# A hybrid encoder layer on one core: how the row maxima of the attention get from columns into the score product

## The reference, cut to what matters

```
def one_block(qi):                                   # 128 queries
    s = jnp.einsum('bkgqd,bskd->bkgqs', qi, kh)      # scores against all keys
    p = jax.nn.softmax(s, axis=-1)
    return jnp.einsum('bkgqs,bskd->bqkgd', p, vh)
```

## Time and profile before

| | |
|---|---|
| median of three runs | 3463.08 us |
| profiled execution, its own time | 3468.2 us |
| span of its trace | 3466.0 us |
| TensorE matmul busy | 2960.6 us, 85% |
| VectorE busy | 2319.8 us, 67% |
| ScalarE busy | 1557.6 us, 45% |
| GpSimd busy | 582.9 us, 17% |
| mean granted TensorE clock | 0.921 |

### The profile page before, as it was taken

The page is one execution under the profiler, slowest core; times in us unless marked ns, Lnnn a source line. Parts: engine busy times, 40 slices in busy tenths (PEclk is TensorE's granted clock), DMA queues, the critical chain, the costliest instruction groups (busy, mean ns, idle before and its releaser), DMA issues. The chain is left out here.

```text
span 3466.0 us, 42658 instructions
## 1 busy us (share of the span) xinstructions
PE 2960.6 (85%) x13075; PEld 2028.4 (59%) x13075; DVE 2319.8 (67%) x2874; ACT 1557.6 (45%) x1980; POOL 582.9 (17%) x395
## 2 busy tenths in 40 slices
PE   6999999669999999996996499959999999999940
PEld 3666666434444444443664277847777777777730
DVE  2556555427777777774776544458888788888856
ACT  2323322102333333335553223217777777777744
POOL 0000000000000000002893000012323232332335
PEclk8999999768999999998997699969999999999975
DMA  6112111353111101100003433346677776678347
GB/s 245 49 46 63 49 45 47 95 160 86 29 28 36 33 21 36 33 16 7 1 0 128 135 121 124 124 163 253 219 270 264 294 278 237 224 260 314 144 161 313
DMA packets 237754, 446.17 MB, mean 129 GB/s; under 512 B 21377, under 2 KB 95197, under 8 KB 236925
## 3 DMA queue, kind: packets, MB, share of 16 engines
q1 hardware_dynamic: 222277, 397.67, 34.3%
q0 software_dynamic: 15408, 47.73, 3.6%
q10 hardware_dynamic: 8, 0.01, 0.0%
HBM read 367.45 MB, written 86.29 MB: 131 GB/s over the span
## 5 line engine op out<-in xcount | busy, mean ns | idle before, releaser
L2175 DVE TENSOR_TENSOR weights_rest<-w,weights_rounded 128x2048 fp32r<-128x2048 f32 x315 | 716.8, 2289 | 134.8 <-ACT weights_rounded L2108 132.5
L2108 ACT ACTIVATE weights_rounded<-w 128x2048 fp32r x315 | 602.1, 1921 | 171.9 <-PE ps_up L2030 108.4
L832 ACT ACTIVATE probs<-ps_scores 128x1024 f32<-128x1024 f32 x260 | 266.0, 1023 | 506.2 <-PE ps_scores L763 438.6
L855 DVE TENSOR_REDUCE part_max<-ps_max 128x1 f32<-128x512 f32 (+1 forms) x528 | 337.8, 677 | 196.6 <-PE ps_max L740 196.6
L2030 PE MATMUL ps_up<-weights_rounded,block_T_rounded 128*128 128x512 f32 x832 | 339.5, 408 | 32.0 <-DVE block_T_rest L2183 32.0
L425 PE MATMUL ps_proj<-w_in,n1T 128*128 128x512 f32 (+2 forms) x1152 | 348.6, 461 | 6.5 <-PEq L108 6.5
L2030 PE MATMUL ps_up<-weights_rounded,block_T_rest 128*128 128x512 f32 x832 | 327.7, 394 | 0.0
L2030 PE MATMUL ps_up<-weights_rest,block_T_rounded 128*128 128x512 f32 x832 | 326.7, 393 | 0.0
L773 PE MATMUL ps_attn<-probs,v 128*64 128x512 f32 x1040 | 283.6, 625 | 0.0
L425 PEld LDWEIGHTS ps_proj<-w_in,n1T 128*128 128x128 f32 x1152 | 197.8, 193 | 145.5 <-issue 130.4
L740 PE MATMUL ps_max<-kT,q_for_max 128*128 128x512 f32 (+1 forms) x528 | 191.6, 436 | 76.4 <-DVE part_max L855 41.5
(11 more groups left out here) (353 smaller groups left out, 4902.1 us busy)
## 6 DMA issues: line engine op xcount, KB each, us to landing
w<-in_w SPq DMA_DIRECT2D x96, 2048.0 KB, 11.3
expert_rows<-scratch_y SPq DMA_DIRECT2D x36, 512.0 KB, 9.3
w_ada_rest<-in_w_ada SPq DMA_DIRECT2D x5, 2048.0 KB, 15.8
scratch_qT<-qT_stage SPq DMA_DIRECT2D x18, 512.0 KB, 3.5
q_for_max<-scratch_qT SPq DMA_DIRECT2D x36, 256.0 KB, 5.7
q_rounded_twice<-scratch_qT SPq DMA_DIRECT2D x36, 256.0 KB, 4.4
mix_rows<-scratch_mix SPq DMA_DIRECT2D x18, 512.0 KB, 4.9
scratch_h<-h_rows SPq DMA_DIRECT2D x18, 512.0 KB, 2.6
```

What stands on the lines that cost most here:

```text
L832: act.activation(pf[:, slot(p, n), :], ps_s[:, n % 2, :], ACT.Exp).then_inc(exp_done, 1)
L855: nc.vector.tensor_reduce(mx[:, p, n // H, n % H:n % H + 1], ps_m[:, n % 2, 0:PART], AX.X, ALU.max).then_inc(m_taken, 1)
L2108: act.activation(split_piece(wh, s), raw_piece(s, buf[0]), ACT.Copy).then_inc(hi_done, 1)
L2175: nc.vector.tensor_tensor(split_piece(wl, s), raw_piece(s, buf), split_piece(wh, s).bitcast(F32), ALU.subtract).then_inc(lo_done, 1)
```

## The change

The 8 products of `row` become one: all 8 columns of `nm` are the stationary operand at once, and the result is 8 rows (PSUM partitions 64 to 71) of 128 values in one bank, a row per head. `ql` and `kT1` grow from 65 to 72 rows; rows 64 to 71 of `kT1` are ones. In `ql` row 64 + h holds the negated maxima of head h in the columns of head h and zero in those of the other heads, so the sum over 8 rows is what the single row gave. VectorE writes these rows: `spread_max` multiplies the 8x128 values, repeated for 8 heads, by an 8x8 piece of the identity, each value repeated 128 times, and signals `q_ready`. It stands in VectorE's program behind `follow` of step ROW_STEP; before the first tile it stands behind the maxima. ScalarE's `take_row` is gone. The second score product is now 72 rows deep.

```
-            gp.memset(S["kT1"][HD:HD + 1, :, :].bitcast(F32), 1.0).then_inc(zeroed, 1)
+            gp.memset(S["kT1"][HD:HD + NH, :, :].bitcast(F32), 1.0).then_inc(zeroed, 1)
...
-        ql = sb("q_rest_and_max", [HD + 1, 2, NH, P], F32R)
+        ql = sb("q_rest_and_max", [HD + NH, 2, NH, P], F32R)
...
-                for h in range(NH):
-                    last = nc.tensor.matmul(ps_m[HD:HD + 1, h // 4, (h % 4) * P:(h % 4 + 1) * P], nm[:, p, h:h + 1], S["ident"][:, :],
-                                            start=(h % 4 == 0), stop=(h % 4 == 3), skip_group_check=True)
-                last.then_inc(row_ready, 1)
+                nc.tensor.matmul(ps_m[HD:HD + NH, 0, 0:P], nm[:, p, :], S["ident"][:, :], start=True, stop=True).then_inc(row_ready, 1)
...
-            def take_row(t, p):
-                act.wait_ge(row_ready, t + 1)
-                act.activation(ql[HD:HD + 1, p, :, :], ps_m[HD:HD + 1, :, :].rearrange("p b (h n) -> p (b h) n", n=P), ACT.Copy).then_inc(q_ready, 1)
-
...
-            take_row(0, 0)
...
-                    if n == ROW_STEP and not is_last(t):
-                        take_row(t + 1, 1 - p)
...
+            def spread_max(t, p):
+                dve.wait_ge(row_ready, t + 1)
+                own = S["ident"][HD:HD + NH, HD:HD + NH].rearrange("p (h o) -> p h o", o=1).to_broadcast([NH, NH, P])
+                nc.vector.tensor_tensor(ql[HD:HD + NH, p, :, :], ps_m[HD:HD + NH, 0, 0:P].rearrange("p (o n) -> p o n", o=1).to_broadcast([NH, NH, P]),
+                                        own, ALU.mult).then_inc(q_ready, 1)
...
+            spread_max(0, 0)
...
+                    if n == ROW_STEP and not is_last(t):
+                        spread_max(t + 1, 1 - p)
...
-            sb("kT1", [HD + 1, NKV, T], F32R, stack=mixer)
+            sb("kT1", [HD + NH, NKV, T], F32R, stack=mixer)
```

## The result

| | median us | runs | ratio to before, 95% |
|---|---|---|---|
| before | 3463.26 | 4 (3461.39 to 3464.26) | |
| after | 3437.22 | 4 (3434.42 to 3438.24) | 0.992 [0.9907, 0.9932] |

The change takes 26.0 us; 25.6 had been forecast (3437.5 us, range 3431 to 3448). The profiled execution after took 3434.42 us (span 3432.5 at a mean clock of 0.922), 2.8 us under its median, while that of before lay 4.9 over its own (5.1 over the median of three). So the two profiles stand 33.8 us apart, and only the stage of the change is compared between them.

A forecast was written before the change was run, and what follows sets the result against it. TensorE's own program was taken to pace the sample's attention. 22.9 us at 15 boundaries plus 2.7 at the first tile made 25.6, from 3463.1 to 3437.5 us, range 3431 to 3448.

The forecast's parts named there:

- 14 passes fewer at 0.109 us: TensorE's row at the sample's 15 tile boundaries: 16 passes become 2, 1.53 us saved each, 22.9 us in all.
- Rival (d): Row product at boundaries: start and end cost more than columns, 0.5 us more each, gain 18, 3445 us; chance 0.07.
- The spread at 1.22 us, hidden: VectorE's new spread at the 15 boundaries: 1.22 us, ending 0.8 us before the next score needs it, costing nothing.
- Rival (a): VectorE's spread costs double, as in the scan (2.24 us): gain 20.1 us, 3443.0 us; chance 0.1.
- The first tile: Start of the sample's attention, in series at half clock: 2.94 us fewer passes, 0.21 more for the spread, net -2.7.
- the clock: Sample's first tile: the rise from 1.2 to 2.4 GHz moves with the work; if it stayed, 1.2 us given back.
- The prompt at 0: Prompt's attention: its second tile waits for its queries' transfer anyway, so shorter rows save 0.
- Depth at 0: 512 second score products grow from 65 to 72 rows deep: costs 0, with ends at 0 and +1 us.
- ScalarE's copy at 0: 18 row copies of 1.02 us leave ScalarE, idle 64% of the stage: worth 0.
- Rival (b): Behind the attention, something fixed in time eats most of the gain, leaving 0 to 7 us: 3460 us; chance 0.05.
- Rival (c): At boundaries, spread and wake-up take over 3.6 us and bound the path to `q_ready`: slower, 3470 us; chance 0.03.

The follow-up runs named there:

- Experiment 3: The changed kernel with its one row product issued eight times, repeats writing the same values; 3461.24 us, before 3462.81.
- experiment 1: The kernel before with its eight products, but the row's copy moved from ScalarE to VectorE; 3460.79 us, before 3462.81.
- experiment 4: The changed kernel with the spread done twice, the second waiting for the first; 3447.95 us, before 3462.81.
- experiment 5: The changed kernel, but the prompt's attention keeps the eight products and ScalarE's copy; 3434.76 us, before 3462.25.
- experiment 2: The kernel before with only the second score product made 72 rows deep, the seven new query rows zero; 3460.13 us, before 3462.81.
- experiment 9: The kernel of experiment 8 with the sample's spread ahead of VectorE's add at ROW_STEP instead of behind it; 3387.59 us, before 3462.69.
- companion: The kernel of experiment 8 run once more on the same chip as experiment 9; 3389.04 us, before 3462.69.
- experiment 8: The changed kernel with the sample's third maximum product behind `weigh` on TensorE, VectorE keeping all reductions ahead of the add; 3389.46 us, before 3462.25.
- experiments 7: The changed kernel with the sample's third maximum product behind `weigh` on TensorE and its reduction behind VectorE's add; 3402.64 us, before 3462.25.

## Why the prediction was right, step by step

The forecast of 25.6 us holds as a median (26.0) and, more tellingly, in its terms.

- **14 passes fewer at 0.109 us**: 22.9 forecast, 15 x 1.52 = 22.8 in the traces. Experiment 3 gives the passes back and with them the gain; experiment 1 does it from the other side. Rival (d) is out: a row of two passes holds TensorE for 0.32 us, the 1.84 less 1.52.
- **The spread at 1.22 us, hidden**: 1.222 measured, 0.82 to spare at the score (0.8 forecast), 1.05 us of VectorE's idle time left (1.08 forecast). Rival (a) is out by the row, and experiment 4 shows that its price was right in kind: twice as long, it costs 0.62 us a boundary. Its size was low: the prediction took the whole 0.8 us as room and counted 0.2 to 0.3 a boundary for a spread of 2.24 us. With the 0.63 us that experiment 4 shows it would be 2.24 - 1.22 - 0.63 = 0.39, an estimate, and 5.9 us in all instead of 4.5. Nor is it the repeated operand that makes the scan's row dear: in the kernel before, the same row takes between 1224 and 2802 ns. What makes it so stays open.
- **The first tile**: -2.7 forecast. In series it was -2.77; up to the first boundary's row the stretch went from 50.30 to 47.33 us, -2.97. The step that rested on an assumption is the clock: I had it move with the work. In after it did nearly (6.1 us behind the first score, 6.6 before), and that is worth the 0.2. Experiments 1 and 3 show that this was luck and no law (last section): there it rose ahead of the first score, and the same stretch came out 2.5 us shorter with no product saved.
- **The prompt at 0**: the same start of the second tile, and experiment 5.
- **Depth at 0**: experiment 2. **ScalarE's copy at 0**: experiment 1, where taking it off ScalarE changes no period.
- **Rival (b), given back later**: not here, with the median 0.3 us from what the stage lost. But something of the kind exists: in experiment 9 the scan took 5.4 us more than its companion's, from a cause that stays open. For a gain of 8 us a chance of 0.05 would be too low.
- **Rival (c), the way to `q_ready`**: not here. Its mechanism showed in experiment 8 once TensorE's row moved nearer to the maxima.

What I had seen and passed over was the larger prize: the 35.3 us of the earlier trace rows, which a change in the order of one product takes away: experiment 8 stands 46.8 us under after.

## What to carry to other kernels

Where an engine sets the pace, count what its program holds at the repeated boundary, by starts of neighbours (1.84 us) and not by busy times (1.91 or 288 x 0.27), and multiply by the boundaries. Then ask of the new work on another engine two things, both read from one timeline: when its last input comes in that engine's order, and when the consumer wants it; 0.8 us between the spread's end and the score, 0.6 of it usable, made this spread free, and twice the spread cost 11 us. A wait that the list names with a count and a steady size (57 times 0.6 us) is an ordering question before it is an engine question: moving one product behind the next independent one was worth more (46.8 us) than the change itself (26.0).

## What the runs showed of the hardware

**TensorE's clock at the sample's first tile does not follow the work alone.** Before, the row of 3.57 us without a pause, from 793.10, was followed by half clock until about 804.5. Experiment 1 has the same 16 passes in the same place, and its first score is at full clock already:

```profile
790.93 3.57 PE L747 MATMUL ps_max<-ident,neg_max 128*1 128x128 f32 x16 [1.01 <-DVE neg_max L852]
795.91 0.47 PE L762 MATMUL ps_scores<-q_rounded_twice,kT 128*128 128x512 f32 x1 [1.41 <-DVE q_rest_and_max L856]
```

Experiment 3 shows the same pair (3.58, then 0.47). In the other kernels the rise from 1.2 to 2.4 GHz came 3.5 to 6.6 us behind the first score. Between the sample's first row and the first boundary's row the stretch was 47.76 us in experiment 1 against 50.30 before, though the way to the first score was 0.21 us longer: 50.30 - 47.76 + 0.21 = 2.75 us from the clock alone, as much as the forecast's whole term for this tile. One profile of each does not show how often it falls which way. The Trainium skill ("TensorE: Matmul & The Clock Gate", on what is actually happening) says that the beat of the chip's look at activity runs freely, so that the place of the rise varies from run to run, by 500 ns either way. These traces agree that the place varies, but by far more: in the four kernels with the same row of 16 passes the rise lay 4.1 and 4.2 us (experiments 3 and 1), 8.3 us (experiment 2) and 11.4 us (before) behind the row's start, 7 us apart. In all four a pause of 1.2 to 1.4 us followed the row, and in the first two the rise fell into it.

**A wait in front of an in-order engine can be free.** VectorE waited 33.7 us in all for the old row in experiment 1, and the time did not move. In the other direction, keeping the reductions ahead of the adds was worth 0.51 us a tile (experiments 7 and 8), which I had expected to cost or to do nothing.

**The scan's phase has two lengths**, 257 to 259 and 262 to 264 us, in kernels that do the same work there, one profile of each but two of the kernel of experiment 8, both at 257.3. Whether it is the clock alone is open, and a gain of under 6 us ahead of it can be hidden by it (experiment 9) or made to look larger (experiment 8).
